# A hybrid encoder layer on one core: the order of operand work at four seams of the program

## The chip, the cores and the metric

The kernel runs as one launch on one core of a Trainium2 chip. The time is device microseconds from start to end of the program; 2913.25 us is the median of three runs (2906.82 to 2917.03). The engines are PE (matrix products), ACT, DVE and POOL (elementwise work), and SP, which here only issues DMAs.

## The reference, cut to what matters

One layer over 2048 tokens of width 1024, all in float32. The four seams of this case lie in its second half:

```python
x = x + mix @ w_out[l]
h = rmsnorm(x, g_cross[l])
x = x + memory_cross_attention(h, rmsnorm(mem, g_mem[l]), w_cq[l], w_ckv[l], w_co[l])
h = rmsnorm(x, g_ffn[l])
x = x + (jax.nn.silu(h @ w_gate[l]) * (h @ w_up[l])) @ w_down[l]
return rmsnorm(x, g_final)
```

Cross-attention has 4 heads of 256 into 256 memory tokens; the feed-forward width is 2816.

## The kernel before

**Split operands.** A float32 product is made of three reduced-precision ones (`split3`, lines 51 to 53): high by high, low by high, high by low. So every operand is needed as a high part, which ACT makes by a copy into the narrower type, and a low part, which DVE or POOL makes by subtracting the high part from the original. "Operand work" is this: a DMA lands the raw tile, ACT copies, DVE or POOL subtracts, PE multiplies.

**Order.** There is no scheduler. Each engine runs its own list, written out in program order (`@block.scalar` for ACT, `@block.vector` for DVE, `@block.gpsimd` for POOL, `@block.tensor` for PE, `@block.sync` for SP). Semaphores join the lists. An instruction that waits holds up all that stands behind it on its engine. Cross-attention, gate-up and the last stage share one block, so an engine passes from one to the next without a barrier.

**Cross-attention** (`stage_cross`). 16 token tiles of 128 rows. For tile n PE transposes the tile (`turn_x2`, L2076), forms scores (48 matmuls in two banks), transposes the softmax output (`turn_probs`, L2100), forms the output (`outputs`, 48 matmuls), and later transposes the normalized result (`turn_x3`, L1809). ACT makes the high part of the turned tile (`x2_high`, L1922), the sum of squares (`square_x2`, `square_x3`), the exponentials (`exps`, L1932), the high parts of the second weight (`n_high`, L1959) and the copy of the turned result (`ffn_input`, L1953). DVE makes the low parts (`x2_low` L1999, `probs_low` L2026), the maxima, the residual (`residual`, L2034) and the scaled result (`scale`, L2041). The block's list on DVE opens with a wait for the norm's gain, which SP loads by DMA at the start of the stage. POOL makes the norm factors, the low parts of the weight (`n_low`, L1871) and, for each pair of tiles, four differences of the copied results (`mix_pair`, L1787 to L1792), which a Strassen-like scheme wants.

**Gate-up** (`stage_gate_up`). Seven products per weight pair instead of eight (`N_PROD = 7`), two halves of the tokens (`HALVES`), eleven pairs (`FP`), gate and up: 308 products of 12 matmuls, counted by s. Product s is number q = s mod 7 of weight block kp = s div 7, and it uses accumulator s mod 8. Its token operand t(q) is loaded and split once in each half (`t_high` on ACT, L2368, and `t_low` on DVE, L2416, each in two parts of 1024 columns). The weight operands are split once per product: high parts by ACT (`w_high`, L2362), low parts by POOL for q = 0, 1, 4 (`low`, L2336) and by DVE for q = 2, 3, 5, 6 (`w_low`, L2409). Four of the seven weights are sums that POOL forms first (`sums`, L1659 to L1664). The sums of block kp+1 overwrite those of block kp, so POOL waits until DVE has split all four. The operands of the first three products are made ahead, on the last tiles of cross-attention (`ahead.*`, L1668 to L1697). At s = 3 PE first does the last `turn_x3`. The half switch is at s = 154: products 154 to 160 need the seven new token operands. After each pair's up block DVE forms four mixtures of the activations (`mix`, L2281 to L2286), which SP stores.

**The last stage** (`stage_down`). Seven products (p) of eight units (u), 33 matmuls each, counted by e = 8p + u. For every new p eleven weight tiles are split: ACT high, POOL low for even tiles (`low`, L2685), DVE low for odd ones. In the last two products each finished unit is normalized: ACT squares (L2743), POOL forms the factor (`factor`, L2691 and L2694), DVE scales (L2793). A unit can be finished as soon as its last product is added.

## Time and profile before

| | us |
|---|---|
| median of three runs | 2913.25 |
| the profiled execution | 2910.78 |
| its span, first to last instruction | 2909.0 |
| granted TensorE clock, mean | 0.979 of full |

The profile is of one execution. Its span leaves 1.8 us of the execution's time outside. A timeline row reads: start, duration, engine, line, operation, output and inputs, shape, count; a bracket at its end gives the idle time of that engine just before and what ended it. In a row with a count over 1 the duration is that of the whole run of instructions. SPq is SP issuing DMAs. PE's matmul rows overlap, since matmuls are pipelined.

### The profile page before, as it was taken

How to read it: one execution, taken by the hardware profiler on the slowest of the kernel's cores; microseconds unless marked ns; L12 is line 12 of the kernel's file. 1: busy time of each engine (PE TensorE's matmuls, PEld its weight loads, DVE VectorE, ACT ScalarE, POOL GpSimd, SP SyncE). 2: the span in 40 equal slices, each digit the busy share in tenths (PEclk: the TensorE clock that was granted, in tenths of full speed). 3: DMA queues.
4: the chain of work that ended last, by engine and by line, in shares of the span. 5: the costliest groups of instructions: out<-in, count | busy, mean ns of one | idle time of the engine just before them, and what ended most of it. 6: DMA issues, size and time to landing. Idle time of an engine off the chain costs nothing.

```text
span 2909.0 us, 39405 instructions
## 1 busy us (share of the span) xinstructions
PE 2778.0 (95%) x14112; PEld 2349.5 (81%) x14112; DVE 1593.9 (55%) x2913; ACT 1063.5 (37%) x2101; POOL 1057.9 (36%) x754
## 2 busy tenths in 40 slices
PE   7999999699999899899999899999999999999998
PEld 7887788599999788688887688888788887788876
DVE  3246546367789433233334766666766666554364
ACT  5433333256666322333332433334233333222342
POOL 6644444210000111312122645554555553452242
PEclk9999999899999999899999899999999999999999
DMA  7757676556655434222224433335333334644453
GB/s 239 253 181 240 198 250 224 151 153 167 170 130 124 167 130 159 86 75 73 85 75 155 144 108 95 109 105 177 106 109 109 109 105 163 239 146 145 143 173 122
DMA packets 244536, 428.48 MB, mean 147 GB/s; under 512 B 17792, under 2 KB 151424, under 8 KB 239104
## 3 DMA queue, kind: packets, MB, share of 16 engines
q1 hardware_dynamic: 211040, 364.72, 39.5%
q10 hardware_dynamic: 33312, 61.35, 7.0%
q8 instruction: 109, 1.79, 0.3%
q14 instruction: 75, 0.61, 0.1%
HBM read 285.50 MB, written 135.27 MB: 145 GB/s over the span
## 4 chain that ended last, share of the span: by engine, by line
PE 59%; DVE 2%; DMA 2%; ACT 1%; SPq 1%; issue 1%; POOL 0%; POOLq 0%; DVEq 0%; ACTq 0%
PE gu_acc L51 9%; PE gu_acc L53 9%; PE gu_acc L52 9%; PE down_acc L51 4%; PE down_acc L53 4%; PE down_acc L52 4%; PE cross_sum_s L51 2%; PE cross_sum_s L53 2%; PE cross_sum_s L52 2%; PE cross_sum_o L51 2%; PE cross_sum_o L53 2%; PE cross_sum_o L52 2%; PE mix_acc L53 2%; PE mix_acc L52 2%; PE mix_acc L51 2%; DVE gu_t L2416 1%
## 5 line engine op out<-in xcount | busy, mean ns | idle before, releaser
L51 PE MATMUL gu_acc<-gu_t,shared_m 128*128 128x512 f32 x704 | 276.0, 392 | 13.2 <-DVE shared_m L2409 7.1
L52 PE MATMUL gu_acc<-gu_t,shared_m 128*128 128x512 f32 x704 | 275.5, 391 | 0.0
L53 PE MATMUL gu_acc<-gu_t,shared_m 128*128 128x512 f32 x704 | 275.5, 391 | 0.0
L337 POOL TENSOR_TENSOR front_wq_lo<-front_wq_raw,front_wq_hi 128x1024 fp32r<-128x1024 f32 x72 | 179.2, 2490 | 208.4 <-ACT front_wq_hi L333 208.4
L1437 PE MATMUL att_sum_o<-att_v,att_turned_sb 128*128 128x64 f32 x1616 | 203.0, 270 | 0.0
L1437 PEld LDWEIGHTS att_sum_o<-att_v,att_turned_sb 128*128 128x128 f32 x1616 | 197.1, 193 | 0.3
L2362 ACT ACTIVATE shared_m<-kept_x 128x512 fp32r<-128x512 f32 x175 | 109.6, 629 | 213.6 <-PE gu_acc L53 194.4
L1407 PE MATMUL att_sum_s<-att_k,att_q 128*128 128x320 f32 (+3 forms) x704 | 146.3, 327 | 25.6 <-DMA att_k<-qk_d 24.7
L51 PEld LDWEIGHTS gu_acc<-gu_t,shared_m 128*128 128x128 f32 x704 | 133.2, 189 | 41.5 <-DVE shared_m L2409 7.4
L52 PEld LDWEIGHTS gu_acc<-gu_t,shared_m 128*128 128x128 f32 x704 | 133.3, 189 | 27.7
L53 PEld LDWEIGHTS gu_acc<-gu_t,shared_m 128*128 128x128 f32 x704 | 133.0, 189 | 27.8
L333 ACT ACTIVATE front_wq_hi<-front_wq_raw 128x1024 fp32r<-128x1024 f32 x72 | 76.2, 1058 | 200.0 <-PE qkv_acc L53 142.9
L51 PE MATMUL gu_acc<-shared_m 128*128 128x512 f32 x352 | 138.3, 393 | 3.4 <-POOL shared_m L2336 3.4
L53 PE MATMUL gu_acc<-shared_m 128*128 128x512 f32 x352 | 138.0, 392 | 0.0
L52 PE MATMUL gu_acc<-shared_m 128*128 128x512 f32 x352 | 138.0, 392 | 0.0
L1344 DVE CUSTOM_DVE_ANT_0 att_scores<-att_sum_s,att_bias 128x640 f32<-128x640 f32 (+4 forms) x128 | 94.9, 741 | 61.0 <-PE att_sum_s L1407 45.1
L1407 PEld LDWEIGHTS att_sum_s<-att_k,att_q 128*128 128x128 f32 x704 | 103.4, 194 | 26.4 <-issue 20.0
L2336 POOL TENSOR_TENSOR shared_m<-kept_x,shared_m 128x512 fp32r<-128x512 f32 x66 | 104.1, 1590 | 47.0 <-ACT shared_m L2362 47.0
L51 PE MATMUL qkv_acc<-front_h,front_wq_hi 128*128 128x512 f32 x288 | 114.8, 399 | 4.6 <-PEq L90 4.6
L2336 POOL TENSOR_TENSOR shared_m<-ahead_w_even,shared_m 128x512 fp32r<-128x512 f32 x64 | 84.9, 1342 | 89.8 <-ACT shared_m L2362 89.8
L51 PE MATMUL qkv_acc<-qkv_h,front_wq_hi 128*128 128x512 f32 x288 | 115.4, 401 | 0.0
L53 PE MATMUL qkv_acc<-qkv_h,front_wq_lo 128*128 128x512 f32 x288 | 114.2, 397 | 0.0
(334 smaller groups left out, 7640.8 us busy)
## 6 DMA issues: line engine op xcount, KB each, us to landing
front_wq_raw<-in_w_in ACTq DMA_DIRECT2D x69, 512.0 KB, 3.8
ahead_w_even<-in_w_gate SPq DMA_DIRECT2D x44, 512.0 KB, 4.4
kept_x<-in_w_up SPq DMA_DIRECT2D x44, 512.0 KB, 4.4
a_d<-gu_a_mix SPq DMA_DIRECT2D x88, 256.0 KB, 3.2
att_k<-qk_d SPq DMA_DIRECT2D x36, 512.0 KB, 13.2
a_d<-gu_a SPq DMA_DIRECT2D x66, 256.0 KB, 4.2
kept_x<-in_w_down SPq DMA_DIRECT2D x56, 256.0 KB, 4.7
shared_m<-a_d SPq DMA_DIRECT2D x19, 704.0 KB, 4.5
```

Source lines behind the costliest of these rows:

```text
L51: pe.matmul(out, l_hi, r_hi, start=first, stop=False)
L52: pe.matmul(out, l_hi, r_lo, start=False, stop=False)
L53: return pe.matmul(out, l_lo, r_hi, start=False, stop=last)
L333: act.activation(self.hi[:, i % Q_SLOTS, :], self.raw[:, i % Q_SLOTS, :], ACT.Copy).then_inc(self.s_hi, 1)
L337: pool.tensor_tensor(self.lo[:, i % Q_SLOTS, :], self.raw[:, i % Q_SLOTS, :], raw(self.hi[:, i % Q_SLOTS, :]), ALU.subtract).then_inc(self ...
L1344: last = dve.tensor_tensor_reduce(out=to, in0=from_, in1=add, scale=1.0, scalar=start, op0=ALU.add, op1=ALU.max, accum_out=top[:, u % 4, x ...
L1407: last = pe.matmul(sum_s[u % 2][:, x * BANK + bank:x * BANK + bank + b - a], qs, k_t[part][:, k_slot(J), key0 + a:key0 + b], start=part == ...
L1437: last = pe.matmul(sum_o[u % 2][:, x * HD:(x + 1) * HD], turned_sb[:, u % 2, first:first + P], v_t[:, k_slot(J), i + 1 - w + y, :], start= ...
L2336: pool.tensor_tensor(w_lo[:, s % RS, :], w_source(s), raw(w_hi[:, s % RS, :]), ALU.subtract).then_inc(s_wlo_a, 1)
L2362: act.activation(w_hi[:, s % RS, :], w_source(s), ACT.Copy).then_inc(s_whi, 1)
L2416: dve.tensor_tensor(t_lo[q][:, cols], raw(t_lo[q][:, cols]), raw(t_hi[q][:, cols]), ALU.subtract).then_inc(s_tlo, 1)
```

## The change

It reorders, and adds no arithmetic. In the order of the program:

1. Cross-attention, first tile: ACT copies the first turned tile (`x2_high(0)`) before it squares it; DVE's wait for the gain moves from the head of its list to the first `scale`; ACT splits two weight tiles before the first exponentials and six behind them, where it was four and four.
2. Cross-attention, last tiles: PE does `turn_x3(14)` behind `outputs(15)`, not in front of it. The copy of the last tile's result, `ffn_input(15)`, leaves cross-attention's list.
3. First gate-up block: ACT makes the four weight high parts q = 3 to 6 first, then t(3), then `ffn_input(15)`, then t(4) to t(6). DVE makes its three weight low parts before all of t(3) to t(6). POOL makes low(4) before the last `mix_pair`.
4. Half switch: the mixture of pair 10 moves on DVE from the end of s = 153 to the end of s = 156.
5. Last stage, before the last product: POOL makes the low parts of tiles 0 and 2 before it forms the norm factor of the unit in front.

```diff
+        def ffn_input(act, n):
+            r = place["x3", n] % 2
+            if n >= 2:
+                act.wait_ge(s_sth, 7 * 16 * (n // 2))
+                act.wait_ge(s_mixed, 4 * (n // 2))
+            for b in range(2):
+                act.wait_ge(s_x3t, 2 * n + b + 1)
+                act.activation(h[:, n % 2, 4 * b:4 * b + 4, :],
+                               turned[r][b][:, :].rearrange("p (k t) -> p k t", k=4),
+                               ACT.Copy).then_inc(s_h, 1)
...
-            square_x2(0)
             x2_high(0)
+            square_x2(0)
...
                 if n == 0:
-                    for k in range(4):
+                    for k in range(2):
                         n_high(k)
...
                 if n == 0:
-                    for k in range(4, KT):
+                    for k in range(2, KT):
                         n_high(k)
-                if n >= 2:
-                    ffn_input(n - 2)
+                if 2 <= n <= NT:
+                    ffn_input(act, n - 2)
...
         def _(dve):
-            dve.wait_ge(s_gain, 16)
-
...
             def scale(n):
+                if n == 0:
+                    dve.wait_ge(s_gain, 16)
                 dve.wait_ge(s_rs3, n + 1)
...
-                if n >= 2:
+                if 2 <= n < NT:
                     turn_x3(pe, n - 2)
...
                 if 1 <= n <= NT:
                     outputs(n - 1)
+                if n == NT:
+                    turn_x3(pe, n - 2)
...
                 if kp == 0:
+                    low(4)
                     cross.mix_pair(pool, NT // 2 - 1)
...
-                low(kp * N_PROD + 4)
+                    low(kp * N_PROD + 4)
...
             for q in range(3, N_PROD):
+                w_high(q)
+            t_high(0, 3)
+            cross.ffn_input(act, NT - 1)
+            for q in range(4, N_PROD):
                 t_high(0, q)
-                w_high(q)
...
             for q in range(3, N_PROD):
-                t_low(0, q)
                 if q in SUMS:
                     w_low(q)
+            for q in range(3, N_PROD):
+                t_low(0, q)
...
-                if q == N_PROD - 1 and kp % 2 == 1 and s < TOTAL - 1:
+                if q == N_PROD - 1 and kp % 2 == 1 and s < TOTAL - 1 and kp != FP * 2 - 1:
                     mix(dve, kp // 2)
+                if s == TURN0 + N_PROD + 2:
+                    mix(dve, FP - 1)
...
+                last_unit = p + 1 < N_PROD and u == N_UNIT - 1
+                if last_unit:
+                    for pr in range(3):
+                        if not low_by_dve(p + 1, pr):
+                            low(p + 1, pr)
                 if e >= 1 and final_at(e - 1):
                     factor(final_at(e - 1))
...
-                if p + 1 < N_PROD and u == N_UNIT - 1:
-                    for pr in range(FP):
+                if last_unit:
+                    for pr in range(3, FP):
```

ACT at the seam between cross-attention and gate-up, before. The last `square_x3` is the row on cross_junk; gu_t are t(3) to t(6), shared_m the weight high parts:

```order
L1913 ACTIVATE cross_junk,cross_ss<-kept_x 128x1024
L1953 ACTIVATE cross_h<-cross_turned 128x512 x2
L2353 UNCONDITIONAL_BRANCH
L2368 ACTIVATE gu_t<-gu_t 128x1024 x2
L2362 ACTIVATE shared_m<-ahead_w_even 128x512
L2368 ACTIVATE gu_t<-gu_t 128x1024 x2
L2362 ACTIVATE shared_m<-ahead_w_even 128x512
L2368 ACTIVATE gu_t<-gu_t 128x1024 x2
L2362 ACTIVATE shared_m<-kept_x 128x512
L2368 ACTIVATE gu_t<-gu_t 128x1024 x2
L2362 ACTIVATE shared_m<-ahead_w_third 128x512
```

And the same place now:

```order
L1924 ACTIVATE cross_junk,cross_ss<-kept_x 128x1024
L2356 UNCONDITIONAL_BRANCH
L2365 ACTIVATE shared_m<-ahead_w_even 128x512 x2
L2365 ACTIVATE shared_m<-kept_x 128x512
L2365 ACTIVATE shared_m<-ahead_w_third 128x512
L2371 ACTIVATE gu_t<-gu_t 128x1024 x2
L1801 ACTIVATE cross_h<-cross_turned 128x512 x2
L2371 ACTIVATE gu_t<-gu_t 128x1024 x6
```

The four weight copies now stand ahead of everything, and the copy of the last result stands behind t(3).

DVE at the half switch, before. gu_t are the low parts of t(4), then of t(5) and t(6); gu_a_mix is the mixture of pair 10:

```order
L2416 TENSOR_TENSOR gu_t<-gu_t 128x1024 x2
L2472 TENSOR_TENSOR kept_x<-gu_acc,kept_x 128x512
L2425 TENSOR_TENSOR gu_a<-kept_x,gu_gate 128x512
L2281 TENSOR_TENSOR gu_a_mix<-gu_a 128x512
L2282 TENSOR_TENSOR gu_a_mix<-gu_a 128x512
L2284 TENSOR_TENSOR gu_a_mix<-gu_a_mix,gu_a 128x512
L2286 TENSOR_TENSOR gu_a_mix<-gu_a,gu_a_mix 128x512
L2416 TENSOR_TENSOR gu_t<-gu_t 128x1024 x4
L2449 TENSOR_TENSOR gu_gate<-gu_acc,kept_x 128x512
```

And now:

```order
L2422 TENSOR_TENSOR gu_t<-gu_t 128x1024 x2
L2478 TENSOR_TENSOR kept_x<-gu_acc,kept_x 128x512
L2431 TENSOR_TENSOR gu_a<-kept_x,gu_gate 128x512
L2422 TENSOR_TENSOR gu_t<-gu_t 128x1024 x4
L2455 TENSOR_TENSOR gu_gate<-gu_acc,kept_x 128x512
L2415 TENSOR_TENSOR shared_m<-kept_x,shared_m 128x512
L2460 TENSOR_TENSOR kept_x<-gu_acc,kept_x 128x512
L2283 TENSOR_TENSOR gu_a_mix<-gu_a 128x512
L2284 TENSOR_TENSOR gu_a_mix<-gu_a 128x512
L2286 TENSOR_TENSOR gu_a_mix<-gu_a_mix,gu_a 128x512
L2288 TENSOR_TENSOR gu_a_mix<-gu_a,gu_a_mix 128x512
```

The four mixtures stand behind t(5), t(6), two combinations and one weight low part.

POOL before the last product of the last stage, before. down_ms and down_rs are the norm factor, the L2685 rows the low parts of tiles 0, 2, then 4 and 6, then 8 and 10:

```order
L2679 TENSOR_TENSOR down_t_raw<-down_t_raw,kept_x 128x512
L2691 TENSOR_SCALAR down_ms<-down_ss 128x1
L2694 TENSOR_TENSOR down_rs<-down_ms,down_power 128x1
L2685 TENSOR_TENSOR shared_m<-ahead_w_even,shared_m 128x512
L2685 TENSOR_TENSOR down_t<-ahead_w_even,down_t 128x512
L2685 TENSOR_TENSOR shared_m<-kept_x,shared_m 128x512 x2
L2685 TENSOR_TENSOR shared_m<-down_t_raw,shared_m 128x512 x2
```

And now:

```order
L2688 TENSOR_TENSOR down_t_raw<-down_t_raw,kept_x 128x512
L2694 TENSOR_TENSOR shared_m<-ahead_w_even,shared_m 128x512
L2694 TENSOR_TENSOR down_t<-ahead_w_even,down_t 128x512
L2700 TENSOR_SCALAR down_ms<-down_ss 128x1
L2703 TENSOR_TENSOR down_rs<-down_ms,down_power 128x1
L2694 TENSOR_TENSOR shared_m<-kept_x,shared_m 128x512 x2
L2694 TENSOR_TENSOR shared_m<-down_t_raw,shared_m 128x512 x2
```

Two of the six low parts have moved in front of the factor; four still stand behind it.

## Rows read from the trace of the kernel before

**Rows 1.** The page, part 1: busy time of each engine.

```profile
PE 2778.0 (95%) x14112; PEld 2349.5 (81%) x14112; DVE 1593.9 (55%) x2913; ACT 1063.5 (37%) x2101; POOL 1057.9 (36%) x754
```

**Rows 2.** Waits of PE: us in total, times, longest.

```profile
PE att_sum_s L1407 <- DMA att_k<-qk_d: 24.7, 2, 19.6
```

**Rows 3.** Timeline of the start of cross-attention, several engines.

```profile
1175.73 1.26 PE L2076 MATMUL cross_turned<-kept_ident,kept_x 128*128 128x128 f32 x8 [2.63 <-PEq L90]
1176.61 1.06 ACT L1922 ACTIVATE beside_turned<-cross_turned 128x512 fp32r<-128x512 f32 x2
1180.92 1.29 DVE L1999 TENSOR_TENSOR beside_turned<-cross_turned,beside_turned 128x512 fp32r<-128x512 f32 x2 [7.09 <-DMA cross_gain<-in_g_ffn]
1182.27 0.80 PE L51 MATMUL cross_sum_s<-shared_m,beside_turned 128*128 128x512 f32 x1 [5.28 <-DVE beside_turned L1999]
1197.03 3.89 ACT L1959 ACTIVATE cross_n<-cross_n 128x1024 fp32r<-128x1024 f32 x4
1202.16 0.76 PE L51 MATMUL cross_sum_s<-shared_m,beside_turned 128*128 128x512 f32 x1 [5.77 <-ACT cross_probs L1932]
1203.69 14.86 POOL L1871 TENSOR_TENSOR cross_n<-cross_n 128x1024 fp32r<-128x1024 f32 x6
1218.12 0.51 PE L51 MATMUL cross_sum_o<-cross_n,beside_turned 128*128 128x512 f32 x1 [0.70 <-DVE beside_turned L2026]
```

**Rows 4.** Windows: length; busy and count of PE, PEld, DVE, ACT, POOL; PEclk; DMA, GB/s.

```profile
1182.90:1185.90 3.00, 3.00 (x9) 2.33 (x8) 0.00 (x0) 0.00 (x0) 0.00 (x0) 0.50 1.02 431
1188.30:1191.30 3.00, 3.00 (x15) 2.47 (x14) 0.69 (x1) 0.00 (x0) 0.00 (x0) 1.00 0.50 210
...
2047.30:2050.20 2.90, 2.87 (x7) 2.32 (x8) 2.90 (x3) 0.00 (x0) 0.00 (x0) 0.50 0.79 228
```

**Rows 5.** Timeline from the last tiles of cross-attention into gate-up.

```profile
1571.99 1.29 DVE L2026 TENSOR_TENSOR beside_turned<-cross_turned,beside_turned 128x512 fp32r<-128x512 f32 x2 [0.43 <-ACT beside_turned L1942]
1576.61 8.97 DVE L1697 TENSOR_TENSOR shared_m<-shared_m 128x1024 fp32r<-128x1024 f32 x4
1576.74 1.97 PE L1809 MATMUL cross_turned<-kept_ident,cross_xn 128*128 128x128 f32 x8 [5.04 <-DVE cross_xn L2041]
1600.25 1.09 ACT L1953 ACTIVATE cross_h<-cross_turned 128x512 f32<-128x512 f32 x2 [5.63 <-PE cross_turned L1809]
1602.31 3.66 DVE L2416 TENSOR_TENSOR gu_t<-gu_t 128x1024 fp32r<-128x1024 f32 x2 [5.29 <-ACT gu_t L2368]
1607.70 0.80 PE L51 MATMUL gu_acc<-gu_t,shared_m 128*128 128x512 f32 x1 [7.14 <-DVE shared_m L2409]
1608.74 2.26 POOL L2336 TENSOR_TENSOR shared_m<-ahead_w_even,shared_m 128x512 fp32r<-128x512 f32 x1
1617.91 1.29 POOL L1659 TENSOR_TENSOR kept_x<-kept_x 128x512 f32<-128x512 f32 x1 [6.91 <-DVE shared_m L2409]
1623.12 4.64 POOL L2336 TENSOR_TENSOR shared_m<-kept_x,shared_m 128x512 fp32r<-128x512 f32 x3
1624.89 0.79 PE L51 MATMUL gu_acc<-shared_m 128*128 128x512 f32 x1 [3.38 <-POOL shared_m L2336]
```

**Rows 6.** Timeline of the half switch of gate-up.

```profile
2038.28 1.66 DVE L2281 TENSOR_TENSOR gu_a_mix<-gu_a 128x512 f32<-128x512 f32 x1
2044.90 5.68 DVE L2416 TENSOR_TENSOR gu_t<-gu_t 128x1024 fp32r<-128x1024 f32 x4
2047.33 0.76 PE L51 MATMUL gu_acc<-gu_t,shared_m 128*128 128x512 f32 x1 [6.10 <-DVE gu_t L2416]
2057.00 1.30 POOL L1659 TENSOR_TENSOR kept_x<-ahead_w_even 128x512 f32<-128x512 f32 x1 [2.73 <-DVE shared_m L2409]
```

**Rows 7.** Timeline before the last product of the last stage.

```profile
2831.88 0.39 POOL L2691 TENSOR_SCALAR down_ms<-down_ss 128x1 f32<-128x1 f32 x1 [6.57 <-ACT down_junk L2743]
2834.60 0.76 PE L51 MATMUL down_acc<-shared_m 128*128 128x512 f32 x1 [4.63 <-POOL shared_m L2685]
2836.64 3.91 POOL L2685 TENSOR_TENSOR shared_m<-kept_x,shared_m 128x512 fp32r<-128x512 f32 x2
```

More of the change, by code:

```diff
@@ L1698, in t_low @@
                               ALU.subtract).then_inc(self.s_tlo, 1)
-CrossEnd = namedtuple("CrossEnd", "put mix_pair turn_x3 s_stx s_sth s_xn s_exp s_o s_x3 s_x3t s_h")
+CrossEnd = namedtuple("CrossEnd", "put mix_pair ffn_input turn_x3 s_stx s_sth s_xn s_exp s_o s_x3 s_x3t s_h")
 GateUpEnd = namedtuple("GateUpEnd", "store_plain store_mixed mix consumed total s_prod s_st")
@@ L1944, in probs_high @@
                                    ACT.Copy).then_inc(s_phi, 1)
-            def ffn_input(n):
-                r = place["x3", n] % 2
-                if n >= 2:
-                    act.wait_ge(s_sth, 7 * 16 * (n // 2))
-                    act.wait_ge(s_mixed, 4 * (n // 2))
-                for b in range(2):
-                    act.wait_ge(s_x3t, 2 * n + b + 1)
-                    act.activation(h[:, n % 2, 4 * b:4 * b + 4, :],
-                                   turned[r][b][:, :].rearrange("p (k t) -> p k t", k=4),
-                                   ACT.Copy).then_inc(s_h, 1)
             def n_high(k):
@@ L1959, in n_high @@
                 act.activation(n_sb[0][:, k, :], raw(n_sb[1][:, k, :]), ACT.Copy).then_inc(s_nhi, 1)
+            x2_high(0)
             square_x2(0)
-            x2_high(0)
             for n in range(NT + 2):
@@ L2120, in _ @@
                     scores(n)
-                if n >= 2:
+                if 2 <= n < NT:
                     turn_x3(pe, n - 2)
@@ L2128, in _ @@
                     outputs(n - 1)
+                if n == NT:
+                    turn_x3(pe, n - 2)
                 if n < NT:
                     turn_probs(n)
-        return CrossEnd(put, mix_pair, turn_x3, s_stx, s_sth, s_xn, s_exp, s_o, s_x3, s_x3t, s_h)
+        return CrossEnd(put, mix_pair, ffn_input, turn_x3, s_stx, s_sth, s_xn, s_exp, s_o, s_x3, s_x3t, s_h)
 N_PROD = 7
```

## The prediction, made before the changed kernel ran

> **What bounds the kernel now.** I read the page's first part first: PE is busy for 95% of the span, the other engines for 55% or less [rows 1]. So the time is PE's work plus PE's gaps, and a change of order can only win gaps. Next the waits of PE: the largest is 24.7 us on key loads of the earlier attention [rows 2], which the change does not touch. Then the timeline at each seam that the diff names. There stand seven gaps of PE, each in the bracket of the matmul that ends it: 5.28 and 5.77 at the start of cross-attention [rows 3], 5.04, 7.14 and 3.38 at its end and the start of gate-up [rows 5], 6.10 at the half switch [rows 6], 4.63 before the last product [rows 7]. That is 37.3 us. Between these seams PE runs without a gap worth counting, so a us won at a seam is a us off the end, as long as nothing new is late.
>
> A gap costs more than its length. After the one that ends at 1182.27 the granted clock is 0.50 of full, 1.2 GHz; from 1188.3 it is full, 2.4 GHz [rows 4]. Nine matmuls touch 3.00 us at half and fifteen at full; with two overlapping the edges that is 0.43 and 0.23 us from start to start, so a slow matmul loses 0.20. Slow lasts at least from 1182.3 to 1185.9 and is over by 1188.3, 8 to 14 matmuls: a restart costs 1.7 to 2.8 us, near 2. At the half switch about seven are slow, 1.4 us [rows 4].
> The Trainium skill (TensorE: Matmul & The Clock Gate, Part 1) says that the number of slow matmuls after a start varies from run to run, with 6, 11 and 14 seen for one kernel. This trace agrees in kind; by that rule each restart that stays costs 1.2 to 2.8.
>
> **Start of cross-attention.** DVE's first low part begins at 1180.92, and its bracket says that it waited 7.09 us for the gain, which nothing needs before the first scale many us later. ACT's two copies, 1.06 us, end by 1177.7 already now, though the square stands ahead of them; so the swap on ACT itself is worth 0.1 at most, since PE's transposes run until 1176.99. DVE can start on the first copy at about 1177.1 and needs 1.29 for both: 1178.4. PE starts there, not at 1182.27: 3.9 won. The clock is down there in either case, since it had an idle PE on both sides of the transposes; if it is not, 2 more. Bounds 3.5 to 5.9.
> The 5.77 gap is ended by ACT's exponentials, which stand behind four weight splits of 3.89 together [rows 3]. Two of the four go: 3.89 / 2 = 1.9 won, bounds 1.9 to 3.9, the upper if the shorter gap of 3.8 keeps the clock. What is late next are the weight low parts on POOL. The last six take 14.86 from 1203.69, so end at 1218.55, and PE starts to use them at 1218.12, the eighth only after seven times three matmuls, 4.8 us later. That leaves 4.3; POOL moves with the first 3.9, not with the 1.9, so 2.4 remain and the order costs nothing. The square that now comes behind the copies feeds the factor that DVE's maxima want after 48 matmuls; nothing waits.
>
> **End of cross-attention and start of gate-up.** Today PE stands 5.04 us for the scaled tile 14 and then transposes it at 1576.74 at half clock, in front of `outputs(15)`. The operand of that product is ready when DVE ends at 1571.99 + 1.29 = 1573.3 [rows 5]. So PE does 48 matmuls from 1573.35 to 1584.2 (48 x 0.227). This pulls everything of PE's forward by some 6 us, but the next user is what counts. The copy of tile 14 on ACT, and t(1) behind it, now wait for the transposes at 1584.2. Two of DVE's four low parts that took 8.97 move behind that, and the residual of tile 15 stands behind them. So of the 6 us I let 1.0 through to the residual, the load of t(3) that SP issues behind it, and the last copied result (estimate, 0 to 2).
> From there the end is set on POOL, as the 3.38 gap says. Now: the result is copied by 1600.25 + 1.09 = 1601.3; `mix_pair` runs until 1608.74; low(4) takes 2.26; POOL idles 6.91 until DVE has split the last summed weight, which stands behind all of t(3) to t(6); sums from 1617.91 to 1623.12, low(7), PE at 1624.89. With the change low(4) goes in front (2.26 won, hidden in POOL's idle time before the copy) and the weight low parts stand in front on DVE, so the 6.91 goes too: 9.2. Against it the sums now lie beside DVE's low parts of t(5) and t(6). A POOL operation takes 1.29 alone and 2.26 beside DVE [rows 5]; I let two of four be so: 1.9 lost. 9.2 + 1.0 - 1.9 = 8.3 won at s = 7. Lower bound: all four at 2.26 (3.9 lost) and nothing from the residual, 5.3. Upper: no contention and 2, 11.2.
> PE must have four products ready by then: 48 x 0.227 = 10.9 plus at most 2.8 of slow clock, 13.7. s = 7 would start at 1616.6, so s = 3 has to start by 1602.9. Its operands: t(3) now stands on ACT directly in front of the copy that ends at about 1600.3, and on DVE nothing stands between. PE starts near 1600, not at 1607.70. The 7.14 gap shrinks to about 3 and no longer decides. What is queued behind new waits: `ffn_input(15)` now holds t(4) to t(6) on ACT if the transposes are late; PE does them after s = 2, at about 1595, so it doesn't. DVE still waits for the stores of the last mixtures before its first combination; these move with POOL, and PE needs that combination only nine products later.
> GPSIMD Engine Reference of the Trainium skill (Key points) says that POOL shares its memory interfaces with DVE and that the two contend when DVE reads two operands in SBUF. The low parts of t are such. If that held for every POOL operation in this stretch the term would be the lower bound, 5.3; the trace agrees with the rule where they overlap and does not say how many will.
>
> **Half switch.** The mixture of pair 10 holds DVE from 2038.28 to 2044.90; behind it the low parts of t(5) and t(6), and PE waits 6.10 for the first of them. Without the gap PE would go on at 2041.23. With the slow matmuls gone too: 6.1 + 1.4 = 7.5. The four low parts would start at 2038.28; PE takes one per half product, 1.36 us, at 2041.2, 2042.6, 2044.0 and 2045.3. They run beside POOL's sums. At 1.83 each (3.66 for two) the last is ready at 2045.6, 0.3 late; at 2.24 (8.97 for four) at 2047.2, 2 late [rows 5]. So 7.2 or 5.5; I take 6.7, since POOL finishes during the last ones. The mixture then takes DVE for 3 us if POOL rests and 6.6 if not, as today. Behind it stand the low parts of the next weights and, through them, POOL's sums, today at 2057.00 with PE's product s = 168 some 16 us later. Sums and first low part take 7 of these (5.2 and 1.8, as at the start of gate-up), so 9 are spare. PE comes 6.7 earlier and the sums stay within 2 us of where they are: some 2 in hand, and none if they come later. Also DVE's first product of pair 11 waits for the mixtures' stores, now some 8 us later; PE needs nothing of it for eight accumulators. Cost 0, or 2 if both run long. Bounds 4 to 7.5.
>
> **Last product.** POOL idles 6.57 before the factor at 2831.88, that is from 2825.3, while its low parts for tiles 0 and 2 could be made: done by 2829.8 even at 2.26, and PE is free at 2834.60 - 4.63 = 2829.97. But low(4) still stands behind the factor, which ACT's square releases. PE does tiles 0 to 3 in 12 x 0.227 = 2.7 and stands at 2832.7. Today the first low part begins about 1.4 before PE's start, at 2833.2; now low(4) does, ready at 2834.5. Then two at 1.95 (3.91 for two) and one of 1.3: 2839.7. PE ends tile 10 at 2840.4. Today it ends at 2834.60 + 33 x 0.227 + 2 = 2844.1. That is 3.7; broken into waits the clock may fall, which cost 1.5. I take 3.0, bounds 2 to 3.9. Of the gap most turns into a smaller wait on the same engine.
>
> **Sum.** 3.9 + 1.9 + 8.3 + 6.7 + 3.0 = 23.8. The profiled execution took 2910.78, which gives 2887.0; it lies 2.5 below the median of the runs, which gives 2889.4. I say 2888. All low ends give 2894, all high ends 2878 from the same base.
>
> **Rivals.**
> Contention and queues take back half: POOL's sums at 2.26 in gate-up (3 less), DVE's low parts and mixture late at the half switch (3 less), 2894. For it: the doubled durations beside the other engine [rows 5]. Against: POOL has pauses at both places [rows 5, 6].
> Another operand paces gate-up: t(3) lands no earlier than now and DVE's queue, freed of the wait, is filled by something that I don't see, so that s = 7 comes at 1624.89 as before: 8.3 less, 2896. For it: the residual moves by 1 us only. Against: idle POOL time in front of the sums is shown as waiting on that one DVE operation.
> Shorter gaps spare restarts: cross-attention's start twice, 4 us more, 2884. For it: the gap falls from 5.28 to 1.4. Against: two restarts' worth of idle time on either side remain.
> The other side: the clock. The change makes long gaps into chains of short ones. If the granted clock then fell at 1573 and stayed at 1.2 GHz, each matmul loses 0.20. From 165 slow ones more than now (33 us) the kernel is over 0.3% slower: outputs(15), seven products of gate-up and the next three do it, 2920. Against: no stretch of rows 4 stays slow beyond 14 matmuls.
> The Trainium skill (same page and part) reports a clock monitor seen stuck at a low rate for over 50 us; no row here shows such.
>
> **How the numbers follow.** Forecast 0.70, contention 0.14, another pace 0.06, spared restarts 0.07, the clock 0.02, and 0.01 that all seams together give under 9 us. The spread of the three runs, 10 us, adds about 4 to either side, so the range is 2878 to 2899. A measurement here tells a change from none at about 0.3%, 8.7 us; faster then needs 2904.5. Four cases lie clear of that, except that noise takes 0.05 of the two slower ones: faster 0.92, same 0.06, slower 0.02.
>
> **What would show it.** In the profile after: first scores of cross-attention about 1.4 us behind the transposes, the next gap 3.8; `outputs(15)` 1.6 behind `turn_probs(15)`, at full clock; POOL without idle time between `mix_pair` and the sums, and PE's s = 7 ended by POOL's low(7); no gap over 1.5 at s = 159; before the last product a first wait of under 0.5 and one of about 2 inside it, ended by POOL. Wrong would be: a gap of PE over 3 us at any place that has none now, DVE's first product of pair 11 holding up a weight low part that PE waits for, or a slow clock beyond 20 matmuls.

## The result and the profile after

| | before | after |
|---|---|---|
| median, us | 2913.25 | 2891.47 (2889.75 to 2896.44, 5 runs) |
| profiled execution, us | 2910.78 | 2892.82 |
| its span, us | 2909.0 | 2891.0 |
| granted clock, mean | 0.979 | 0.983 |

The ratio of the times is 0.9928, with a 95% interval from 0.9912 to 0.9945. The prediction said 2888 (2878 to 2899).

The first part of the page after. It answers [rows 1]: the same work on every engine, within 0.7% of before, in a shorter span.

```profile
PE 2777.0 (96%) x14112; PEld 2345.9 (81%) x14112; DVE 1598.6 (55%) x2913; ACT 1062.6 (37%) x2101; POOL 1064.3 (37%) x754
```

The waits of PE after, as in [rows 2]. The largest rests of the seams stand in the last three rows; each of the others is 2.5 us or less in total:

```profile
PE att_sum_s L1407 <- DMA att_k<-qk_d: 24.8, 2, 20.1
...
PE down_acc L51 <- DVE beside_turned L2786: 5.4, 2, 4.2
PE gu_acc L51 <- DVE gu_t L2422: 5.0, 7, 1.9
...
PE down_acc L51 <- POOL shared_m L2694: 4.0, 4, 1.3
PE cross_sum_s L51 <- ACT cross_probs L1943: 3.9, 1, 3.9
```

The longest wait of the row above them (down_acc, 4.2) is at no seam of the diff. It comes up below.

**The start of cross-attention**, timeline after, answering [rows 3]:

```profile
1178.41 1.34 PE L2076 MATMUL cross_turned<-kept_ident,kept_x 128*128 128x128 f32 x8 [2.62 <-PEq L90]
1179.71 1.40 DVE L1997 TENSOR_TENSOR beside_turned<-cross_turned,beside_turned 128x512 fp32r<-128x512 f32 x2 [3.19 <-ACT beside_turned L1933]
1181.16 0.80 PE L51 MATMUL cross_sum_s<-shared_m,beside_turned 128*128 128x512 f32 x1 [1.41 <-DVE beside_turned L1997]
1196.04 2.00 ACT L1959 ACTIVATE cross_n<-cross_n 128x1024 fp32r<-128x1024 f32 x2
1199.28 0.54 PE L51 MATMUL cross_sum_s<-shared_m,beside_turned 128*128 128x512 f32 x1 [3.87 <-ACT cross_probs L1943]
1214.51 0.50 PE L51 MATMUL cross_sum_o<-cross_n,beside_turned 128*128 128x512 f32 x1 [0.70 <-DVE beside_turned L2024]
```

DVE now starts on ACT's copy (bracket), not on the gain. The gaps are 1.41 and 3.87 where they were 5.28 and 5.77. The first transposes stand 2.7 us later than in the profile of before: the stages in front, which the change doesn't touch, took that much longer in this profile.

**End of cross-attention and start of gate-up**, answering [rows 5]:

```profile
1569.64 0.50 PE L51 MATMUL cross_sum_o<-cross_n,beside_turned 128*128 128x512 f32 x1 [1.63 <-DVE beside_turned L2024]
1590.53 1.29 POOL L2338 TENSOR_TENSOR shared_m<-ahead_w_even,shared_m 128x512 fp32r<-128x512 f32 x1
1595.33 1.06 ACT L1801 ACTIVATE cross_h<-cross_turned 128x512 f32<-128x512 f32 x2
1595.98 0.77 PE L51 MATMUL gu_acc<-gu_t,shared_m 128*128 128x512 f32 x1 [1.94 <-DVE gu_t L2422]
1596.48 1.65 POOL L1787 TENSOR_TENSOR cross_mixed<-cross_h 128x512 f32<-128x512 f32 x1 [4.66 <-ACT cross_h L1801]
1604.79 2.27 POOL L1659 TENSOR_TENSOR kept_x<-kept_x 128x512 f32<-128x512 f32 x1
1607.13 2.15 POOL L1661 TENSOR_TENSOR kept_x<-kept_x 128x512 f32<-128x512 f32 x1
1609.24 2.27 POOL L1662 TENSOR_TENSOR kept_x<-kept_x 128x512 f32<-128x512 f32 x1
1611.59 1.27 POOL L1664 TENSOR_TENSOR ahead_w_third<-kept_x 128x512 f32<-128x512 f32 x1
1614.59 0.50 PE L51 MATMUL gu_acc<-shared_m 128*128 128x512 f32 x1 [2.51 <-POOL shared_m L2338]
```

`outputs(15)` starts 1.63 behind turn_probs(15). low(4) lies in POOL's idle time and takes 1.29. From mix_pair on POOL has no idle time and the sums follow at once. But beside DVE's low parts mix_pair takes 8.3 (1596.48 to 1604.79), where it took 7.3, and three of the four sums take 2.15 to 2.27. POOL still ends the wait of s = 7.

**Half switch and last product**, answering [rows 6, 7]:

```profile
2026.00 8.99 DVE L2422 TENSOR_TENSOR gu_t<-gu_t 128x1024 fp32r<-128x1024 f32 x4
2037.21 0.68 DVE L2283 TENSOR_TENSOR gu_a_mix<-gu_a 128x512 f32<-128x512 f32 x1
...
2812.30 1.29 POOL L2694 TENSOR_TENSOR down_t<-ahead_w_even,down_t 128x512 fp32r<-128x512 f32 x1
2815.73 0.50 PE L51 MATMUL down_acc<-shared_m 128*128 128x512 f32 x1 [0.24 <-DVE shared_m L2781]
2819.26 0.50 PE L51 MATMUL down_acc<-shared_m 128*128 128x512 f32 x1 [1.18 <-POOL shared_m L2694]
2821.49 0.50 PE L51 MATMUL down_acc<-shared_m 128*128 128x512 f32 x1 [0.56 <-POOL shared_m L2694]
2824.10 0.49 PE L51 MATMUL down_acc<-shared_m 128*128 128x512 f32 x1 [0.95 <-POOL shared_m L2694]
```

At the half switch DVE needs 8.99 for the four low parts beside POOL, yet no gap of PE is over 0.55. Before the last product the 4.63 became 0.24, 1.18, 0.56 and 0.95.

**A ledger.** PE does the same matmuls in every version, but for fills that are named. So I took the start of a numbered matmul in each profile and read the seams as stretches between two of them:

- A: first transposes of cross-attention to `outputs(0)`.
- B7, B9: first scores of tile 15 to s = 7, and to s = 9, when the slow matmuls are over.
- C: s = 154 to s = 162 (half switch).
- D: last matmul of gate-up to unit 5 of the last stage.
- E: last matmul of unit 47 to the first of unit 50 (last product).
- T: first transposes of cross-attention to PE's last matmul.

A slow matmul, in what follows, is one of 128x512 that takes more than 0.5 us in the timeline: at 1.2 GHz the rows show 0.63 us, at 2.4 GHz 0.39. The first and the last of a stretch can lie between, so a count is good to one.

The long stretches of gate-up between them agree to 0.01 us (from s = 9 to 154: 394.39 or 394.40 in every profile). From `outputs(0)` to tile 15 they take 329.7 to 329.9 (331.8 in x_n0), and between D and E 330.2 to 332.4. Each row is one profile; the median is of all its runs:

| kernel | A | B7 | B9 | C | D | E | T | median |
|---|---|---|---|---|---|---|---|---|
| before | 42.4 | 77.0 | 85.2 | 29.5 | 45.0 | 22.1 | 1720.7 | 2913.3 |
| after | 36.1 | 70.4 | 77.6 | 23.0 | 47.9 | 19.3 | 1700.0 | 2891.5 |
| u_gain | 40.4 | 70.4 | 76.1 | 23.1 | 44.3 | 19.4 | 1699.1 | 2894.5 |
| u_turn | 36.4 | 70.6 | 76.2 | 24.3 | 44.2 | 19.4 | 1696.7 | 2894.3 |
| u_wlow | 36.5 | 72.9 | 81.3 | 23.2 | 43.0 | 19.4 | 1699.7 | 2895.1 |
| u_low4 | 36.1 | 73.6 | 79.0 | 25.4 | 44.0 | 19.9 | 1700.6 | 2899.4 |
| u_mix | 36.1 | 70.5 | 77.6 | 31.4 | 42.9 | 19.4 | 1703.9 | 2896.4 |
| x_end | 36.4 | 70.5 | 76.0 | 24.1 | 42.5 | 19.5 | 1695.1 | 2891.3 |
| x_fill | 34.8 | 70.4 | 77.5 | 24.0 | 45.7 | 20.0 | 1698.7 | 2891.9 |
| x_n0 | 33.3 | 70.4 | 77.5 | 22.8 | 44.2 | 20.3 | 1696.4 | 2894.1 |
| x_last | 36.4 | 71.0 | 76.6 | 23.1 | 43.2 | 17.9 | 1693.6 | 2884.7 |
| x_resid | 36.1 | 71.4 | 76.8 | 24.4 | 43.6 | 19.4 | 1696.4 | 2892.6 |
| x_best | 33.8 | 71.4 | 76.8 | 24.7 | 41.5 | 19.2 | 1694.3 | 2884.8 |
| x_three | 34.6 | 70.4 | 77.4 | 24.7 | 41.2 | 17.8 | 1692.4 | 2887.1 |

How far one profile can be trusted, seam by seam: among the profiles that share the changed kernel's order at a seam, A differs by 0.4 us, B7 by 0.7, B9 by 1.6, C by 2.6, D by 5.0 and E by 0.9. Of the kernel before there is one profile. The medians were taken beside further runs of the kernel before, whose own medians went from 2910.6 to 2915.1; so medians of two rows compare to a few us only.

Before to after, in us won: A 6.3, B9 7.6, C 6.5, E 2.8, D minus 2.9, all else 0.4: 20.7 in T. The stages in front took 2.7 longer, so 18.0 in the span.

### The profile page after: what moved, and what is told of

The parts are those of the page before. It is cut to its first block, busy times and chain, and to the rows that moved or that the text cites. A ratio compares the mean times of both kernels' runs of the same rounds, so it can differ in the third digit from the quotient of the medians.

```text
span 2891.0 us, 39405 instructions
## 1 busy us (share of the span) xinstructions
PE 2777.0 (96%) x14112; PEld 2345.9 (81%) x14112; DVE 1598.6 (55%) x2913; ACT 1062.6 (37%) x2101; POOL 1064.3 (37%) x754
## 4 chain that ended last, share of the span: by engine, by line
PE 53%; DVE 2%; DMA 1%; ACT 1%; POOL 1%; issue 0%; SPq 0%; POOLq 0%; DVEq 0%; ACTq 0%
PE gu_acc L51 9%; PE gu_acc L53 9%; PE gu_acc L52 9%; PE down_acc L51 4%; PE down_acc L53 4%; PE down_acc L52 4%; PE cross_sum_s L51 2%; PE cross_sum_s L53 2%; PE cross_sum_s L52 2%; PE cross_sum_o L51 2%; PE cross_sum_o L53 2%; PE cross_sum_o L52 2%; DVE gu_t L2422 0%; PE cross_turned L2100 0%; PE cross_turned L1820 0%
## 5 line engine op out<-in xcount | busy, mean ns | idle before, releaser
L53 PEld LDWEIGHTS gu_acc<-gu_t,shared_m 128*128 128x128 f32 x704 | 132.4, 188 | 27.8
L333 ACT ACTIVATE front_wq_hi<-front_wq_raw 128x1024 fp32r<-128x1024 f32 x72 | 76.2, 1058 | 203.9 <-PE qkv_acc L53 156.2
L51 PE MATMUL qkv_acc<-qkv_h,front_wq_hi 128*128 128x512 f32 x288 | 115.3, 400 | 0.0
L52 PE MATMUL qkv_acc<-qkv_h,front_wq_hi 128*128 128x512 f32 x288 | 114.4, 397 | 0.0
```

The costliest lines, as they stand in the source:

```text
L51: pe.matmul(out, l_hi, r_hi, start=first, stop=False)
L52: pe.matmul(out, l_hi, r_lo, start=False, stop=False)
L53: return pe.matmul(out, l_lo, r_hi, start=False, stop=last)
L333: act.activation(self.hi[:, i % Q_SLOTS, :], self.raw[:, i % Q_SLOTS, :], ACT.Copy).then_inc(self.s_hi, 1)
```

## Experiments

The changed kernel with one edit undone (u_), then with something added (x_). A loss of 4 us is inside the interval of a ratio here, so the ledger decides and the median is only shown beside it.

**u_gain.** The wait for the gain alone.

```diff
+            dve.wait_ge(s_gain, 16)
             def x2_low(n):
...
             def scale(n):
-                if n == 0:
-                    dve.wait_ge(s_gain, 16)
```

> The changed kernel with one edit taken back: DVE's wait for the gain stands again at the head of its list. In the profile of the changed kernel the first matmul of the scores comes 1.5 us behind the end of the transposes. My theory: DVE's first low part comes again as late as the gain's DMA lets it, as before (first scores 5.3 behind the transposes), the clock there is down in either case, so the loss is 3.9 us and no more: about 2895.4. Rival: the longer idle time also costs another spell at 1.2 GHz, 2 us more, 2897.4; or the gain lands sooner than in the one profile of before, and the loss is under 2.

The timeline of u_gain:

```profile
1183.80 1.29 DVE L1999 TENSOR_TENSOR beside_turned<-cross_turned,beside_turned 128x512 fp32r<-128x512 f32 x2 [7.20 <-DMA cross_gain<-in_g_ffn]
1185.14 0.79 PE L51 MATMUL cross_sum_s<-shared_m,beside_turned 128*128 128x512 f32 x1 [5.59 <-DVE beside_turned L1999]
```

A grows by 4.3, from 36.1 to 40.4 (profiles that share the order of A lie between 36.1 and 36.5). That the clock was down there in either case holds: 11 slow matmuls behind the gap of 1.41, 13 behind that of 5.59. The rest of A's gain, 42.4 minus 40.4, is 2.0. No run undoes the two weight splits alone; the gap that they stood in front of went from 5.77 to 3.88 in u_gain, which fits.

**u_turn.** PE's order alone.

```diff
-                if 2 <= n < NT:
+                if n >= 2:
                     turn_x3(pe, n - 2)
...
-                if n == NT:
-                    turn_x3(pe, n - 2)
```

> The changed kernel with PE's order at the end of cross-attention taken back: turn_x3(14) stands again in front of outputs(15). All orders of ACT, DVE and POOL stay changed. My theory: what paces gate-up's start is POOL's chain (copy of the last result, mix_pair, sums, low(7)), fed through the residual of tile 15, which DVE reaches only behind the low parts of t(1); turn_x3(14) then comes 8 us earlier and lets ACT and DVE finish those sooner, so the residual moves by about 1 us and s = 7 starts 0 to 2 us later than in the changed kernel, although outputs(15) ends some 6 us later (4.5 of wait and slow matmuls): about 2893. The gap of 5 in front of turn_x3(14) is back, and the wait before s = 3 shrinks in return. Rival: PE's gap counts in full, s = 7 is 5 to 6.6 us later, 2897 to 2898.

PE in u_turn, with the first gap, s = 3 and s = 7:

```profile
1582.00 1.97 PE L1820 MATMUL cross_turned<-kept_ident,cross_xn 128*128 128x128 f32 x8 [5.04 <-DVE cross_xn L2041]
1605.16 0.47 PE L51 MATMUL gu_acc<-gu_t,shared_m 128*128 128x512 f32 x1 [0.62 <-DVE gu_t L2420]
...
1623.77 0.50 PE L51 MATMUL gu_acc<-shared_m 128*128 128x512 f32 x1 [2.52 <-POOL shared_m L2336]
```

The gap of 5.04 is back, the wait before s = 3 shrinks from 1.94 to 0.62, and B7 is 70.6 against 70.4. The eight profiles with the changed order all along B7 have 70.4 to 71.0. So a gap of 5 us on the engine that bounds the kernel was worth 0.2 us here, which is nothing that can be told from the spread.

**u_wlow.** DVE's order at gate-up's start.

```diff
             for q in range(3, N_PROD):
+                t_low(0, q)
                 if q in SUMS:
                     w_low(q)
-            for q in range(3, N_PROD):
-                t_low(0, q)
```

> The changed kernel with DVE's order at gate-up's start taken back: the weight low parts of q = 3, 5 and 6 stand behind the token low parts t(3), t(5) and t(6) again. In the changed kernel POOL's four sums start at 1604.8, take 8.0 us beside DVE's low parts (2.27, 2.15, 2.27, 1.27), and low(7) ends for PE at 1614.6. With the old order DVE has split the last weight about 1.8 us behind its last token part, so at some 1612, and the sums run alone from there at 1.3 each, 5.2: s = 7 starts at about 1618, 3.3 us later, 2895. Rival without the contention: the sums take as long in both, 7 us later, 2898.5. Second rival: DVE's list was never what held the sums, no change, 2891.5.

POOL and PE in u_wlow:

```profile
1614.84 1.30 POOL L1659 TENSOR_TENSOR kept_x<-kept_x 128x512 f32<-128x512 f32 x1 [5.78 <-DVE shared_m L2415]
...
1618.80 1.27 POOL L1664 TENSOR_TENSOR ahead_w_third<-kept_x 128x512 f32<-128x512 f32 x1
...
1621.80 0.79 PE L51 MATMUL gu_acc<-shared_m 128*128 128x512 f32 x1 [3.96 <-POOL shared_m L2338]
```

The sums come 5.3 later and take 1.3 each, not 2.2: s = 7 loses 2.4 (forecast 3.3). POOL's contention with DVE ate about half of what the order won. PE also waits 4.68 before s = 3 in this run, not 1.94, but at s = 7 it waits for POOL again. B9 loses 3.7 to 5.3: behind the gap of 3.96 some 14 matmuls are slow.

**u_low4.** POOL's low(4) behind mix_pair.

```diff
-                    low(4)
                     cross.mix_pair(pool, NT // 2 - 1)
+                    low(4)
```

> The changed kernel with POOL's low(4) back behind the last mix_pair. There it runs beside DVE's token low parts and takes 2.27 us instead of the 1.29 in POOL's idle time. Theory: POOL's chain mix_pair, low(4), sums, low(7) is without idle time, so all 2.27 us count; s = 7 starts 2.2 to 2.3 us later, 72.7 behind the start of the last tile's scores instead of 70.4; in time 2893.5. Rival: PE needs low(4) itself at s = 4, where it is then ready only at about 1607 and holds up products 4 to 6, 3 to 4 us later in all, 2895. Second rival: nothing, POOL is not what s = 7 waits for.

POOL and PE in u_low4:

```profile
1604.07 2.24 POOL L2338 TENSOR_TENSOR shared_m<-ahead_w_even,shared_m 128x512 fp32r<-128x512 f32 x1
1606.41 0.76 PE L51 MATMUL gu_acc<-gu_t,shared_m 128*128 128x512 f32 x1 [6.76 <-issue]
```

B7 is 3.2 longer and the loss is not in POOL's chain alone: PE stands 6.76 at s = 4. The bracket names no releaser ("issue"), but what s = 4 needs and did not have is this very low part, which POOL ends at 1606.31, 0.1 us in front of PE's start. Thirteen matmuls are slow behind it, and PE reaches s = 7 late with no wait there at all. That is the rival. Three of this kernel's four runs lie at 2898.3 to 2900.7, while the profiled one took 2892.9; no profile shows where those 5.5 to 7.8 us went.

**u_mix.** The mixture of pair 10.

```diff
-                if q == N_PROD - 1 and kp % 2 == 1 and s < TOTAL - 1 and kp != FP * 2 - 1:
+                if q == N_PROD - 1 and kp % 2 == 1 and s < TOTAL - 1:
                     mix(dve, kp // 2)
-                if s == TURN0 + N_PROD + 2:
-                    mix(dve, FP - 1)
```

> The changed kernel with the mixture of pair 10 back at the end of s = 153. Theory: DVE's low parts of t(5) and t(6) stand behind 6.6 us of mixing again, PE waits 6 us at s = 159 and runs some seven matmuls at 1.2 GHz behind it: the product count reaches s = 161 6.7 us later, 2898. Rival: most of that wait is taken up by something else that the changed kernel hides behind PE's lead (POOL's sums for the next weights, which end at 2037 there), and the loss is under 4.

DVE and PE in u_mix:

```profile
2025.90 1.67 DVE L2283 TENSOR_TENSOR gu_a_mix<-gu_a 128x512 f32<-128x512 f32 x1
...
2032.52 5.68 DVE L2422 TENSOR_TENSOR gu_t<-gu_t 128x1024 fp32r<-128x1024 f32 x4
...
2034.95 0.77 PE L51 MATMUL gu_acc<-gu_t,shared_m 128*128 128x512 f32 x1 [6.57 <-DVE gu_t L2422]
```

C is 31.4 against 23.0: 8.4 lost, of it 6.57 in the gap; 14 matmuls are slow behind it, seven in the kernel before. Against the other profiles with the changed order, whose C goes up to 25.4, the loss is 6.0 at the least.

**x_end.** The activation load of unit 4 does not wait for the mixtures.

```diff
                 if e == 2:
+                    sp.wait_ge(gate_up.s_st, 16 * (N_PROD * (HALVES * FP - 1) + 3))
+                if e == 6:
                     sp.wait_ge(gate_up.s_st, N_PROD * 16 * HALVES * FP)
                     sp.dma_start(gain[:, :], g_final.to_broadcast([P, D])).then_inc(s_gain, 16)
...
-                if e == 1:
+                if e == 2:
                     gate_up.store_mixed(sp, HALVES * FP - 1)
```

> The changed kernel plus one edit at the start of the last stage: SP issues the activation load of unit 4 as soon as the three plain stores of the last pair have landed, and only then the four stores of the mixtures; it waits for all stores, and loads the gain, at unit 6. In the profiles so far the stretch from gate-up's last product to the fifth unit's second matmul group (147th matmul) takes 38.8 to 43.8 us, where 33.5 would be PE's own work; PE stands 4.2 us for unit 4's load in the changed kernel and up to 13 slow matmuls follow. Theory: that wait is the chain store, wait for seven stores, load, split, so with the load some 8 us earlier it goes, with its slow matmuls; 3.5 to 6 us less, 2886 to 2888. Rival: the mixtures' stores, now later, hold up the loads of the second product's operands or of its weights, and the gap moves to unit 8 or to a weight tile; no gain, 2891.

PE and ACT at the start of the last stage, first in the changed kernel, then in x_end. The ACT row is the copy of unit 4's activations:

```profile
2446.84 0.47 PE L51 MATMUL down_acc<-shared_m,beside_turned 128*128 128x512 f32 x1 [1.21 <-DVE beside_turned L2786]
2470.16 1.38 ACT L2750 ACTIVATE beside_turned<-beside_turned 128x1408 fp32r<-128x1408 f32 x1 [10.58 <-DMA beside_turned<-a_d]
2473.74 0.77 PE L51 MATMUL down_acc<-shared_m,beside_turned 128*128 128x512 f32 x1 [4.21 <-DVE beside_turned L2786]
```

```profile
2449.99 0.76 PE L51 MATMUL down_acc<-shared_m,beside_turned 128*128 128x512 f32 x1 [1.94 <-DVE beside_turned L2788]
2466.82 1.38 ACT L2752 ACTIVATE beside_turned<-beside_turned 128x1408 fp32r<-128x1408 f32 x1 [5.03 <-DMA beside_turned<-a_d]
```

The wait of 4.21 is gone. That alone shows nothing, since u_turn, u_wlow and u_mix, which keep the old order of the load, have no wait there either. What shows the cause is ACT's copy, which waits for the load: it starts 27.8 us behind gate-up's last matmul in x_end (25.8 and 28.1 in x_three and x_best, which have the same edit), and 31.4 to 34.0 in the eleven profiles without it; 34.0 is the changed kernel's own. But the gain is far under the expected 3.5 to 6: D is 42.5, and the ten profiles of the changed kernel and of those that keep its order there have 42.9 to 47.9, 44 in the middle. The 47.9 is the changed kernel's own profile; it lies at the far end. With a spread of 5 us one profile does not tell whether the edit wins anything.

**x_fill.** 14 matmuls whose result nothing uses, in front of the second tile's scores.

```diff
                 if n == 0:
+                    for i in range(14):
+                        pe.matmul(sum_o[0][:, :], m_sb[0][:, 0, 0:P], m_sb[0][:, 0, 0:BANK],
+                                  start=True, stop=True)
                     scores(1)
```

> The changed kernel plus 14 matmuls of 128x512 on old operands, written to a bank of the output that is overwritten later, in front of the second tile's scores: 3 us of work in the 3.9 us in which PE otherwise waits for the exponentials. They add work and their result is used by nothing. Theory that idle time of PE brings the granted clock down: the gap becomes under 1.2 us, the 9 matmuls at 1.2 GHz behind it go, outputs(0) starts 1.5 to 2 us sooner (34.3 behind the first transposes instead of 36.1 to 36.5), 2889.5. Rival: the clock falls at that place whatever PE does there; then the fill itself runs slow, takes up to 6 us and delays the scores by 2, 2893.5.

Two windows behind this wait (start:end, length, busy and count of PE, PEld, DVE, ACT, POOL, then PEclk, DMA share, GB/s), the changed kernel first, then x_fill:

```profile
1199.40:1202.40 3.00, 3.00 (x8) 2.35 (x9) 2.10 (x2) 3.00 (x7) 2.92 (x3) 0.52 0.00 0
```

```profile
1202.50:1205.50 3.00, 3.00 (x13) 2.48 (x14) 2.02 (x2) 3.00 (x7) 2.92 (x3) 1.00 0.02 5
```

The clock is 1.00 where it was 0.52 and no matmul is slow. A is 34.8 against 36.4 (the profiles with the same start), 1.6 less, though PE does 3 us more. It is the idle time that brings the clock down at this place.

**x_n0.** All eight weight high parts behind the exponentials (`range(2)` and `range(2, KT)` become none and `range(KT)`).

> The changed kernel with all eight weight high parts of cross-attention's start behind the first exponentials, none in front. Theory by ACT's queue: the exponentials come 1.9 us sooner, so the second gap is 1.9 instead of 3.9. POOL's low parts now all start 1.9 us later than in front of it and PE uses them one after the other from outputs(0) on: eight at 2.36 from about 1199.5 in the changed kernel's time end at 1219 with the factor between, where PE wants the last at 1214.5 - 1.9 + 4.8 = 1217.4; so nearly all of the 1.9 is lost again to waits between the first matmuls of outputs(0). Forecast: outputs(0) starts 1.9 sooner, its last matmul is 0 to 0.5 sooner: 2891. Rival: POOL is not late and the full 1.9 is kept, or 3.7 with the slow matmuls: 2888 to 2889.5.

PE in x_n0:

```profile
1201.40 0.47 PE L51 MATMUL cross_sum_s<-shared_m,beside_turned 128*128 128x512 f32 x1 [1.99 <-ACT cross_probs L1943]
...
1223.48 0.50 PE L51 MATMUL cross_sum_o<-cross_n,beside_turned 128*128 128x512 f32 x1 [1.35 <-POOL cross_n L1882]
```

The second gap is 1.99 and A 2.8 to 3.2 shorter. The first bank of `outputs(0)` then waits for POOL: from its first to its 48th matmul it takes 12.9 us, otherwise 10.8. About 1 us stays. The choice of two is near the edge of what POOL allows.

**x_last.** Low parts of tiles 0, 2 and 4 before the factor.

```diff
-                    for pr in range(3):
+                    for pr in range(5):
...
-                    for pr in range(3, FP):
+                    for pr in range(5, FP):
```

> The changed kernel with the low parts of tiles 0, 2 and 4 in front of the norm factor before the last product, where it was 0 and 2. In the changed kernel POOL idles 3.0 us in front of that factor, and PE then waits 1.18, 0.56 and 0.95 for tiles 4, 6 or 8 and 10. Theory: tile 4 is made in the idle time, all later ones come 1.8 to 2.2 us sooner, the first unit of the last product takes 2.0 to 2.6 less (9.2 instead of 11.6 from its first matmul to the next unit's): 2889. Rival: the factor comes later, DVE's scaling and low parts with it, and the waits move to DVE: no gain.

PE in x_last:

```profile
2812.95 0.50 PE L51 MATMUL down_acc<-shared_m 128*128 128x512 f32 x1 [1.62 <-DVE shared_m L2781]
2819.84 0.50 PE L51 MATMUL down_acc<-shared_m 128*128 128x512 f32 x1 [0.45 <-POOL shared_m L2694]
```

E is 17.9, 1.5 less (2.0 to 2.6 expected): the wait is now DVE's, whose split of the activations, beside POOL's third low part, took 2.74, where it took 2.16. Its median is 2884.7, ratio 0.9902 (0.9877 to 0.9927).

**x_resid.** The last token tile's chain moved forward: in the order of the diff on ACT (square), DVE, ACT (copy) and PE.

```diff
+                    square_x3(NT - 1)
                     ahead.t_high(act, 1)
...
                     ahead.t_low(dve, 0)
+                    residual(NT - 1)
                     ahead.t_low(dve, 1)
+                    scale(NT - 1)
                     ahead.sum_low(dve)
...
+            cross.ffn_input(act, NT - 1)
             t_high(0, 3)
-            cross.ffn_input(act, NT - 1)
...
-                if s == 3:
+                if s == 2:
                     cross.turn_x3(pe, NT - 1)
```

> The changed kernel with the chain of the last token tile moved forward: DVE adds the residual of tile 15 and scales it around the low parts of t(1), where both stood behind them and behind t(2); ACT squares it in front of t(1) and copies its turned result in front of t(3); PE transposes it before s = 2, not before s = 3. In the changed kernel the residual starts at 1586.34 although outputs(15) ends at 1580.7, and POOL's chain of copy, mix_pair and sums follows from it. Theory: the copy ends at about 1591.3 instead of 1596.4, POOL's chain moves 5 us; DVE, busy nearly without pause from 1583.5 to 1610.4, becomes the bound and its last low part of t(6) moves only 1.5 to 2: s = 7 starts 2.5 to 4 us sooner, 66.5 to 68 behind the start of the last tile's scores; 2888. Rival: DVE's low parts lengthen beside POOL's earlier chain by as much as they gain, no gain, 2891.5.

POOL, DVE and PE in x_resid:

```profile
1597.51 2.22 POOL L1787 TENSOR_TENSOR cross_mixed<-cross_h 128x512 f32<-128x512 f32 x1
1603.55 16.77 DVE L2425 TENSOR_TENSOR gu_t<-gu_t 128x1024 fp32r<-128x1024 f32 x8
1605.98 0.76 PE L51 MATMUL gu_acc<-gu_t,shared_m 128*128 128x512 f32 x1 [5.70 <-DVE gu_t L2425]
```

POOL's chain did start 5.5 sooner, counted from tile 15's scores. But all eight token low parts now lie beside POOL's chain and take 2.10 each (in the changed kernel the first two took 1.18, the others 2.17), and the weight low parts in front 1.76 each, not 0.68. PE stands 5.70 at s = 3 for the first of these token low parts, and at s = 7 it no longer waits for POOL. B7 is 71.4, 1.0 longer. My theory fell; the rival, that DVE's low parts lengthen by as much as the order gains, holds.

**x_best** is x_resid, x_last, x_end and x_fill in one; **x_three** leaves x_resid out. No further edit.

> All that won in the profiles so far, together, on the changed kernel: the last tile's chain moved forward (x_resid), tile 4's low part also in front of the factor (x_last), unit 4's load ahead of the mixtures' stores (x_end), and the 14 matmuls that keep PE busy before the second tile's scores (x_fill; added work whose result nothing uses). By the seams measured one by one: 1.6 of cross-attention's start, 3 of gate-up's start if x_resid does what its theory says, 1.5 of the last product, and 1 to 2 at the start of the last stage: 7 to 8 us under the changed kernel, 2884. Rival: the seams aren't independent, what one gives PE in lead the next wait takes, as where products stand for a load: 2887 or more.

> The changed kernel with three of the four additions of the best version: tile 4's low part ahead of the factor, unit 4's load ahead of the mixtures' stores, and the 14 matmuls that keep PE busy before the second tile's scores; without the earlier chain of the last tile, whose seam measured 1.0 us longer than the changed kernel's. By the seams measured one by one: 1.6 at cross-attention's start, about 2 at the start of the last stage against its usual 44, 0.1 to 1.5 in the last product (19.2 and 17.9 were measured, 19.35 without), and 1.0 back from gate-up's start: 2884 by median, 1 under the version with all four. Rival: the additions that only move a wait (unit 4's load, tile 4) add nothing together, 2889.

Both lie 4 to 7 us under the changed kernel in median: 2884.8, ratio 0.9908 (0.9892 to 0.9923), and 2887.1, ratio 0.9903 (0.9884 to 0.9921); x_last alone did as well. T is 1694.3 and 1692.4. In x_three A, D and E lie 1.8, 2.8 and 1.6 under their usual 36.4, 44.0 and 19.4, so these gains add up there, in one profile. E is 19.2 in x_best, with waits of 1.44, 0.59 and 0.94: what x_last won is not had in every execution. The intervals don't separate the three versions from each other, and all three overlap with that of the changed kernel (0.9912 to 0.9945). That any of them is faster than the changed kernel is likely, not shown.

## Why the prediction was right, step by step

**Cross-attention's start**, said 3.9 + 1.9, measured 4.3 (u_gain) + 2.0 (the rest). The gap of 3.8 did not keep the clock, as taken (9 slow matmuls). x_n0 shows that POOL's spare time, which the term put at 2.4, is real and small: with both splits gone from the front, PE waits 1.35 for POOL.

**End of cross-attention and gate-up's start**, said 8.3, measured 6.6 at s = 7 and 7.6 with the slow matmuls saved. The mis-sized part is the contention. I let two of four sums be slow; three were. And I left out that mix_pair would be slower too: the copied result came 1.3 sooner (said 1.0), but mix_pair took 1.0 longer, so the sums began 9.4 sooner, where 9.2 + 1.0 was said. They took 8.0, where 5.2 + 1.9 was said. The 1.0 between 6.6 and 7.6 is luck: 13 matmuls were slow behind s = 7 before and eight after, which no term counted, and in four other profiles with that gap none were. That PE's early `outputs(15)` would hardly count is confirmed by u_turn. ACT's new order there (the weight high parts first, the last copy behind t(3)) was never undone alone. That low(4) costs only its own time on POOL was wrong in kind: put back, it stops PE at s = 4, which already wants it (u_low4).

**Half switch**, said 6.7, measured 6.5, and 8.4 by u_mix from the other side (6.0 to 8.6 against all profiles with the new order). The four low parts ran at the slow end, 8.99, and PE paid only in waits under 0.55. No cost came of the later mixture.

**Last product**, said 3.0, measured 2.8, in three small waits instead of one of 2; none cost the clock. No run undoes this edit alone; ten profiles with it have 19.3 to 20.3 against the one of 22.1 before.

**The sum**, said 23.8. The seams gave 23.2. What was missing, 2.9, was lost at D, a place that no term named. I had written that PE runs without a gap worth counting between the seams, and at D that was a misreading of the trace of the kernel before: PE waits there twice, and eight matmuls are slow behind the first wait.

```profile
2465.31 0.47 PE L51 MATMUL down_acc<-shared_m,beside_turned 128*128 128x512 f32 x1 [2.54 <-DVE beside_turned L2772]
2491.30 0.47 PE L51 MATMUL down_acc<-shared_m,beside_turned 128*128 128x512 f32 x1 [1.68 <-DVE beside_turned L2772]
```

I had also written that a new gap over 3 us would be a sign of error. There it was, 4.21 instead of 1.68. Unit 4 resumes 37.4 behind gate-up's end before and 37.6 after: the chain of stores and load sets it (x_end). Before, eight slow matmuls were hidden in that wait, and none followed it. After, PE came fast, waited 4.21, and left with 13 slow ones. The nine other profiles with the same order there took 2.2 to 5.0 less, so this belongs to the one profile and is no cost of the change. The median, 21.8 under before, contains the usual mix of it.

**The clock rival** didn't come: no stretch stayed slow beyond 14 matmuls. The forecast of two restarts at cross-attention's start as before holds too.

## What to carry to other kernels

A gap on the engine that bounds the kernel is worth only what the next gap doesn't take back: follow the chain that ends the next wait before you price a gap (5 us were worth 0.2 in u_turn). When two elementwise engines are moved side by side, price both at their contended durations from the start. Where one profile carries the argument, number the matmuls and compare stretches between them; where PE never waits, such stretches agree to 0.01 us, and at a seam profiles of the same order differ by 0.4 to 5.0, while the runs of the kernel before spread over 17. Take more than one profile of a seam before you call a difference of its size a gain.
